# Page requests of the compression stage divided between SyncE and ScalarE

## What is computed

```python
def nsa_compress(kr, pe, w1, w2):
    # rows kr (B,L,G,dh) -> compressed tokens (B,n_cmp,G,dh); block i covers rows [i*16, i*16+32)
    B, L, G, dh = kr.shape
    n = (L - CMP_L) // CMP_S + 1
    r = CMP_L // CMP_S
    chunks = kr[:, :(n + r - 1) * CMP_S].reshape(B, n + r - 1, CMP_S, G, dh)
    blocks = jnp.concatenate([chunks[:, j:j + n] for j in range(r)], axis=2) + pe[None, None, :, None]
    flat = jnp.swapaxes(blocks, 2, 3).reshape(B, n, G, CMP_L * dh)
    return jax.nn.silu(flat @ w1) @ w2

kc = nsa_compress(glob[:, :, 0], pe[0], w1[0], w2[0])
vc = nsa_compress(glob[:, :, 1], pe[1], w1[1], w2[1])
# glob = concatenate([cache_nsa_kv[page_table], new rows])
```

## Time and profile before

| | |
|---|---|
| median of 3 runs | 2987.34 us (2979.53 to 2987.98) |
| profiled execution, its own time | 2986.59 us |
| its span | 2984.8 us |
| PE busy | 2825.6 us, 95% of the span |
| DVE, ACT, POOL busy | 44%, 21%, 16% |
| mean granted PE clock | 0.973 of full speed |
| the first stage | 0 to 362 us |

### The profile page before, as it was taken

One profiled execution on the slowest core, in us unless ns is written; L12 is line 12 of the kernel. 1 busy time (PEld: TensorE's weight loads), 2 busy tenths in 40 slices (PEclk: granted clock), 3 DMA queues, 4 the chain that ended last, 5 costly groups with the idle time before them and its releaser, 6 DMA issues. The chain is left out here.

```text
span 2984.8 us, 42427 instructions
## 1 busy us (share of the span) xinstructions
PE 2825.6 (95%) x15048; PEld 1967.7 (66%) x15048; DVE 1309.1 (44%) x2971; ACT 616.8 (21%) x1521; POOL 486.1 (16%) x355
## 2 busy tenths in 40 slices
PE   8999999998999999899999799999899999999998
PEld 5777777766666655566666566555688888874443
DVE  3111123232642597265665344234566666661321
ACT  2111000001322244244444211244200000010010
POOL 1200100002420344100000100011233333320011
PEclk9999999999999999999999899899899999999999
DMA  7544264435992643531111553300234343405020
GB/s 198 132 87 92 61 195 128 133 102 163 267 275 87 181 153 110 185 90 42 44 37 51 181 165 130 127 29 29 80 118 147 105 145 107 147 16 171 2 85 28
DMA packets 343544, 345.07 MB, mean 116 GB/s; under 512 B 61001, under 2 KB 310025, under 8 KB 341982
## 3 DMA queue, kind: packets, MB, share of 16 engines
q1 hardware_dynamic: 298706, 259.32, 30.1%
q10 hardware_dynamic: 44662, 83.46, 8.6%
HBM read 289.37 MB, written 110.01 MB: 134 GB/s over the span
## 5 line engine op out<-in xcount | busy, mean ns | idle before, releaser
L294 PE MATMUL d_ps<-d_w,mixer_u_T 128*128 128x288 f32 (+2 forms) x2048 | 585.2, 434 | 18.4 <-PEq L145 10.3
L294 PEld LDWEIGHTS d_ps<-d_w,mixer_u_T 128*128 128x128 f32 x2048 | 384.2, 195 | 160.9 <-issue 39.4
L298 PE MATMUL d_ps<-mixer_u_T,d_w 128*128 128x352 f32 x1152 | 397.6, 480 | 20.8 <-DVE d_ob L318 11.3
L298 PEld LDWEIGHTS d_ps<-mixer_u_T,d_w 128*128 128x128 f32 x1152 | 207.3, 194 | 126.9 <-issue 38.1
L3390 PE MATMUL ffn_ps<-ffn_T,up_up_w 128*128 128x264 f32 x704 | 163.8, 386 | 0.0
L318 DVE COPY d_ob<-d_ps 128x288 f32<-128x288 f32 (+3 forms) x144 | 66.4, 462 | 218.0 <-PE d_ps L294 169.7
L3390 PE MATMUL ffn_ps<-up_u_T,ffn_S 128*128 128x264 f32 x672 | 156.4, 386 | 0.0
L3074 PE MATMUL down_Y<-down_w,feed_g_T 128*128 128x512 f32 x352 | 151.9, 593 | 0.0
L3390 PEld LDWEIGHTS ffn_ps<-ffn_T,up_up_w 128*128 128x128 f32 x704 | 133.8, 190 | 22.9
L3390 PE MATMUL ffn_ps<-up_u_T,up_up_w 128*128 128x264 f32 x640 | 145.7, 386 | 0.0
L2882 PE MATMUL mix_B<-gates_o_T,mix_wb 128*128 128x352 f32 x480 | 144.8, 465 | 0.0
(11 more groups left out here) (535 smaller groups left out, 3876.7 us busy)
## 6 DMA issues: line engine op xcount, KB each, us to landing
out_dil_sample<-cache_dil_w ACTq DMA_DIRECT2D x10, 3264.0 KB
up_up_w<-ffn_w_up SPq DMA_DIRECT2D x44, 512.0 KB, 6.0
cmp_rows<-cache_nsa_kv SPq DMA_DIRECT2D x128, 128.0 KB
graw<-d_ob SPq DMA_DIRECT2D x72, 176.0 KB
mix_gate<-graw SPq DMA_DIRECT2D x24, 528.0 KB, 6.1
dils_qb<-proj SPq DMA_DIRECT2D x24, 512.0 KB, 6.7
d_w<-w_in SPq DMA_DIRECT2D x24, 512.0 KB, 6.4
ssd_x<-proj SPq DMA_DIRECT2D x29, 384.0 KB, 4.6
```

Source lines behind the costliest of these rows:

```text
L294: mm = pe.matmul(bank(u)[0:rows, 0:cols], self.u_T[:, k, r0:r0 + rows], self.view(i)[:, k, :], start=(k == 0), stop=(k == DK - 1))
L298: mm = pe.matmul(bank(u)[:, 0:cols], self.view(i)[:, k, x, :], self.u_T[:, k, c * third:(c + 1) * third], start=(k == 0), stop=(k == DK - 1))
```

## The change

The pages of sequences 2 to 7 are asked for by two engines. Of each of the seven parts SP asks for all pages but the last, and ACT, in a lane of its own with the same place and length as `compress`, for the last one: 9 and 7 of 16 pages, so 42 pages move from SP to ACT. Sequences 0 and 1 and the prompt's rows stay with SP. ACT waits for the page table once, and for the same pack as SP.

```diff
@@ -1313,6 +1313,9 @@
+    def pages_of(part):
+        return range(NPAGES * part // SUB, NPAGES * (part + 1) // SUB)
+
     def first_sp(sp):
@@ -1336,11 +1339,24 @@
                 x = n if i < 2 else n + 1
                 part = (i + SUB - 2) % SUB
                 if 2 <= x + 1 < DB:
-                    load(sp, x + 1, range(NPAGES * part // SUB, NPAGES * (part + 1) // SUB))
+                    load(sp, x + 1, pages_of(part)[:-1])
                 elif x + 1 == DB and part == 0:
...
+    def pages_act(act):
+        yield
+        yield
+        for n in range(seqs):
+            for i in range(SUB):
+                x = n if i < 2 else n + 1
+                part = (i + SUB - 2) % SUB
+                if 2 <= x + 1 < DB:
+                    if n == 0 and i == 2:
+                        act.wait_ge(pages_in, 16)
+                    load(act, x + 1, pages_of(part)[-1:])
                 yield
@@ -1489,7 +1505,7 @@
-    return Lane(NPAGES, None, None, None, None, first_sp), Lane(1 + SUB * seqs, pe_program, act_program, dve_program, pool_program, sp_program)
+    return Lane(NPAGES, None, None, None, None, first_sp), Lane(1 + SUB * seqs, None, pages_act), Lane(1 + SUB * seqs, pe_program, act_program, dve_program, pool_program, sp_program)
@@ -4450,10 +4466,10 @@
-                first_pages, compress = compress_lane(nc, own, ins, proj, kc_T, vc, ident, lambda sp: dense.written(sp, 27))
+                first_pages, pages, compress = compress_lane(nc, own, ins, proj, kc_T, vc, ident, lambda sp: dense.written(sp, 27))
...
-                         (compress, 0.115, 0.885), (memory, 0.25, 0.3))
+                         (compress, 0.115, 0.885), (pages, 0.115, 0.885), (memory, 0.25, 0.3))
```

## The result

| | before | changed |
|---|---|---|
| median of 20 runs on one chip | 2983.07 us (2976.85 to 2994.64) | 2995.14 us (2986.29 to 3011.81) |
| profiled execution | 2986.59 us | 2989.16 us |
| next stage's first matmuls | 362.07 us | 369.57 us |

The ratio is 1.0037, 95% interval 1.0023 to 1.0052: the change makes the kernel slower, by about 11 us. PE's busy time is not up; the idle time is.

The account below looks back on a forecast made before the run. PE was taken to bound the kernel, with only its stall for a late pack to win: 6.25 us idle plus 1.46 us slow clock, ACT's cost 0, so 2987.34 - 7.7 = 2979.6 us; range 2974 to 2988 us.

Parts of the forecast that it names:

- What bounds the kernel, and the stall: First stage, PE-bound: SP's issue time makes pack 6 late; 6.25 us idle plus 1.46 us slow clock, 7.7 us.
- The change on SP: SP's queue: nine pages and other work take 22.0 us of PE's 32.65 us, so SP loses nothing.
- What is late next: Sequence 2's pack, behind ACT's last page: done at 132.3, packs about 16.6 us ahead of PE; price nothing.
- The price of a request: Each of ACT's 42 page requests: bounds of 1.0 and 2.3 us, SP's 1.92 us taken.
- the tightest place: Sequence 1 on ACT: copy at 122.55 up to 1.9 us later, cost 0 to 1 us once, taken as 0.
- rival 2: ACT's transpose steps: a 2.3 us request does not overlap the copy; 0 to 5 us lost, 2980 to 2985 us; chance 0.10.
- The change on ACT: ACT's queue: 42 requests fit beside copies in steps of 2.53 us; stores behind requests have slack; cost taken as 0.
- Rival 3: ACT's queue behind `front_w` and weights: requests held 15.4 and 8.93 us; net +14.5 us, 3001.8 us; chance 0.08.

Follow-up runs that it names:

- run 7: The changed kernel, but ACT asks for only two of sixteen pages, one behind each gate, SP for 14: 2981.28 us, ratio 0.9979 to the kernel before.
- run 1: The changed kernel, but the 127-row store of `vc` is split into 112 + 15 rows: 2982.72 us, ratio 0.9985 to the kernel before.
- run 2: The changed kernel, but SP issues the stores of `kc_T` and `vc`, one step into the next sequence: 2984.96 us, ratio 0.9992 to the kernel before.
- run 8: The changed kernel, but ACT asks for only four of sixteen pages, two behind each gate: 2983.94 us, ratio 0.9993 to the kernel before.
- run 6: The kernel before, with only the page behind the stores of `kc_T` and `vc` moved to ACT, six requests in all: 2984.77 us, ratio 0.9997.
- run 5: The changed kernel, but `vc` is stored in three stores of 43, 41 and 43 rows: 3002.13 us, ratio 1.0044 to the kernel before.
- run 10: The changed kernel, with `vc` stored a second time to a scratch tensor that nothing reads: 3017.15 us, ratio 1.0113 to the kernel before.

## Why the prediction was wrong

**What bounds the kernel, and the stall: right.** Pack 6 was late because SP could not issue sixteen pages in PE's time. With two pages off SP (run 7) the wait for pack 6 is gone, as it is in the changed kernel and in runs 1, 2 and 8. In the profiles the 7.7 us are won: run 8's first stage ends 6.2 us early with a 2.9 us wait of its own; run 7's PE is 8.5 us late ahead of sequence 6 (most of it from 65 us, last section) and 0.9 us late behind it. The times show the gain less surely: 0.21% in run 7 (0.03 to 0.39%) where 0.26% was forecast, and in runs 2 and 8 the interval contains no gain too.

**The change on SP: right.** SP now waits for the projection. Its waits in the changed kernel from 100 to 300 us (the kernel before has none there):

```profile
SPq L251 <- ACT d_ob L318: 51.2, 7, 16.7
SPq L251 <- DVE d_ob L318: 27.4, 6, 11.6
```

**What is late next: right that it costs nothing, wrong in size.** The forecast had pack 2 done at 132.3, 16.6 us ahead of PE. It is done at 145.65, 4.3 us ahead. Its last page was asked for at 123.49, about as forecast, but the pack began 17.2 us after that request had gone out, where I took 4.2 us: `front_w`, asked for at 120.64, took 18.9 us to land, with pages and weights beside it. Packs 3 to 6 are 10 to 18.5 us ahead, pack 6 12.9 us.

**The price of a request: nearly right.** Reading the number takes 0.451 us on ACT, the request 1.18 us, with the steps between them 2.07 us against the 1.92 taken. But at the tightest place I took 0 of 0 to 1 us, and PE waits 2.3 us there, for the memory tile, whose Square came at 121.18 instead of 119.98: I had looked at the copies behind the requests, and not at the Square, which feeds DVE and then PE. In run 1, where no request of ACT is held, PE waits 2.0 us there and 1.6 us for the copies of sequences 5 and 6, so rival 2 (0 to 5 us) came true in size beside the larger one.

**The step that failed** is "The change on ACT", in the sentence that the stores of `kc_T`, which sit behind requests, have a whole sequence of slack. I asked what stands behind a request and what it delays, and not what a request stands behind. The sum put this term at 0. The request behind the store of `vc` takes 7.0 and 8.6 us, where a step has room for 2.53. The two cost PE 3.4 and 7.3 us, and 1.9 us of slow clock after the second.

**Rival 3 had the mechanism and not the place.** It said that ACT is held by its queue, that this decides once the hold is over 2.53 us, and gave 14.3 us behind `front_w` and 7.9 us behind weights. `front_w` holds nobody by itself: the page behind it, at 123.49, takes 1.34 us. What holds ACT is the 127-row store while weights or pages are in flight: of the six stores in the changed kernel those at 148 and 254 us are followed by long holds, the second just behind a block of weights, those at 188 and 223 us by none, those at 112 and 293 by 2.6 and 2.3 us. The argument against it, five requests of SP behind weights that were not held, was of a queue without such a store. Its chance of 0.08 was too small: the earlier trace rows had an 8.93 us request on an engine where a hold is free, and the change put requests on one where it is not.

That store is not the only thing that can hold a queue. SP has none in the changed kernel, and its store behind the weights of 128.19, with `front_w` in flight, is held too (run 1: 6.91 us):

```profile
129.50 5.80 SPq L251 DMA_DIRECT2D proj<-d_ob  x1
```

The 8.93 us request of the earlier trace rows stands directly behind the two loads of `cmp_w`; in every profile here the request at that place, at 30 to 35 us, takes 4.9 to 10.7 us. Behind it PE waits at most 1.7 us, for pack 0 at 65 us; behind the hold at 129.50 it waits for nothing. No run tested what holds SP.

**What stays open.** The profiled executions of the changed kernel are among its faster ones. They show +7.5 us in the first stage, the medians +12.1 us. That the typical hold is longer than the profiled ones would fit, but no profile shows it. The rule behind the hold is not shown either: at its end between 11 and 38 rows have gone, not one number. In run 6 the rows' turn comes sooner than at the long holds (at most 5.6 us after the store is asked for, against 6.9 and 8.9), which goes with its milder holds; what brings it sooner was not tested.

## What to carry to other kernels

Before a DMA request is moved to a compute engine, look at the DMA that will stand in front of it in that engine's queue: if its row count has no divisor near 16 (127 rows here) and transfers are in flight, the engine can stand for 7 to 10 us, as here, with its arithmetic in line. Give such a store a row count that divides (112 + 15 here), or leave it to an engine that nobody waits for. Moving only as many requests as the short queue lacks (two of sixteen here, not seven), to places behind the engine's long waits, is enough.

## What the runs showed of the hardware that was not expected

The same request, 8 x 16 rows of 1 KB, takes 0.75 us on SP's queue and 1.18 to 1.21 us on ACT's at the median, in every kernel but run 6, whose six are all held a little.

Part of the difference between profiled executions has a cause of its own, far from the change. At 65 us VectorE scales a tile of 32 x 1024 (L452), in 0.77 us in the changed kernel's profile, in 6.77 us in run 7's. VectorE and GpSimd of run 7:

```profile
65.53 6.77 DVE L452 TENSOR_SCALAR front_x<-front_x,front_ss 32x1024 f32<-32x1024 f32 x1
```

```profile
64.72 7.04 POOL L1378 TENSOR_TENSOR cmp_packed<-cmp_w,cmp_pe_T 128x4096 f32<-128x4096 f32 x1
```

and of the changed kernel:

```profile
64.10 0.77 DVE L452 TENSOR_SCALAR front_x<-front_x,front_ss 32x1024 f32<-32x1024 f32 x1
```

```profile
64.37 7.39 POOL L1378 TENSOR_TENSOR cmp_packed<-cmp_w,cmp_pe_T 128x4096 f32<-128x4096 f32 x1
```

In the profiles of runs 5, 7 and 10 VectorE starts 0.35 to 0.95 us after GpSimd's multiplication and takes 6.6 to 7.2 us, until about 0.5 us after that is over; in the ten others it starts before it and takes 3.2 us at most. PE then waits 4.5 to 5.1 us in the three. This agrees with the Trainium skill, SBUF — State Buffer, section "Who interferes with whom", by which GpSimd and a VectorE instruction in a two-port mode share ports that go to whichever issues first, for its whole instruction; the section names `tensor_scalar` among the instructions that can run so. So a difference of less than 1 us in the order of two engines goes with 4.5 us and more of PE's waiting. No run here changed that order on purpose, so the cause is read from the order alone.
